# Seven row slots and six diagonals in place of eleven and eight in a product-key retrieval pipeline

## What is computed

```
q = (xb @ w_q)                                   # 8 heads, two halves of 128
s = einsum('bhpc,hpnc->bhpn', q, sub_keys)       # 2 x 128 scores for each head
ts, ti = top_k(s, 16); best_s, pos = top_k(all 256 sums, 16)
idx = cand_i[pos];  gate = softmax(best_s)       # 16 experts of 16384
act = gelu(einsum('bhkd,bd->bhk', u_tab[idx], xb))
out = einsum('bhk,bhkd->bd', gate * act, v_tab[idx])
```

## Time and profile before

| What | us |
|---|---|
| Median of three runs | 3976.35 |
| The profiled execution | 3980.32 |
| Its span | 3978.5 |
| PE busy | 2955.1 |
| DVE busy | 2732.4 |
| ACT busy | 1470.4 |
| POOL busy | 1424.2 |
| Mean rate of the DMA engines | 329 GB/s over the span |

### The profile page before, as it was taken

How to read it: one execution, slowest core, us unless ns; L and a number is a source line. 1 busy time by engine, 2 the same in 40 slices (tenths; PEclk the granted TensorE clock), 3 DMA queues, 4 the chain that set the end, 5 groups by cost and what they waited for, 6 DMA issues and landing times.

```text
span 3978.5 us, 56287 instructions
## 1 busy us (share of the span) xinstructions
PE 2955.1 (74%) x20248; PEld 1449.0 (36%) x20248; DVE 2732.4 (69%) x6352; ACT 1470.4 (37%) x4424; POOL 1424.2 (36%) x1272
## 2 busy tenths in 40 slices
PE   5999999868766666777777766788787676666655
PEld 3777777754222122333333322334342222222111
DVE  5555555546766666778777777889867677777775
ACT  1333333313433333444444433444444343333333
POOL 0001110014444444344444444334444444444442
PEclk8888999889787778888889888999998787787777
DMA  2110000039999999999999999999999999999996
GB/s 79 30 30 26 25 25 25 18 111 425 426 426 427 426 427 426 421 416 399 411 404 426 426 426 425 415 353 369 421 394 427 426 425 427 426 426 426 426 426 289
DMA packets 229640, 1311.06 MB, mean 330 GB/s; under 512 B 58736, under 2 KB 61936, under 8 KB 81648
## 3 DMA queue, kind: packets, MB, share of 16 engines
q0 software_dynamic: 165888, 1208.03, 72.6%
q1 hardware_dynamic: 63472, 99.43, 7.1%
HBM read 1301.52 MB, written 5.86 MB: 329 GB/s over the span
## 4 chain that ended last, share of the span: by engine, by line
DMA 36%; PE 19%; DVE 16%; ACT 3%; issue 3%; DVEq 1%; POOL 1%; ACTq 1%; POOLq 0%
DMA arena<-in_uv,arena 36%; DVE arena L1587 8%; PE psum L1159 8%; PE psum L1121 4%; PE psum L1211 3%; PE psum L1241 2%; DVE arena L1674 1%; POOL arena L1101 1%; ACT wbuf L1377 1%; PE psum L1231 1%; ACT arena L1372 1%; DVE arena L1515 1%; DVE arena L1512 0%; ACT arena L1368 0%; DVE arena L1648 0%
## 5 line engine op out<-in xcount | busy, mean ns | idle before, releaser
L1159 PE MATMUL psum<-arena,wbuf 64*64 64x512 f32 (+1 forms) x8704 | 1451.1, 741 | 865.7 <-ACT wbuf L1377 846.3
L1101 POOL DMA_INDIRECT arena<-in_uv,arena x1152 | 1349.7, 1172 | 1770.7 <-PE psum L1159 1569.4
L1587 DVE SCALAR_TENSOR_TENSOR arena<-arena 128x1024 f32<-128x1024 f32 x1152 | 1396.0, 1222 | 584.9 <-DMA arena<-in_uv,arena 569.6
L1159 PEld LDWEIGHTS psum<-arena,wbuf 64*64 64x64 f32 (+1 forms) x8704 | 335.0, 154 | 1755.5 <-ACT wbuf L1377 1379.3
L1368 ACT ACTIVATE arena<-arena 128x2 f32<-128x2 f32 x576 | 117.0, 203 | 1668.1 <-DVE arena L1587 1663.4
L1377 ACT ACTIVATE wbuf<-cst,arena 128x64 f32<-128x64 f32 x1152 | 338.3, 340 | 41.6 <-issue 2.4
L1121 PE MATMUL psum<-arena,wbuf 128*128 128x256 f32 (+1 forms) x1024 | 312.4, 453 | 8.5 <-DVE arena L1598 5.8
L1372 ACT ACTIVATE arena<-arena 128x1 f32<-128x1 f32 x1152 | 276.8, 287 | 40.9 <-issue 1.4
L1121 PEld LDWEIGHTS psum<-arena,wbuf 128*128 128x128 f32 x1024 | 203.9, 210 | 171.5 <-issue 131.2
L842 POOL COPY arena<-arena 128x256 f32<-128x256 f32 x8 | 3.2, 397 | 584.2 <-DVE arena L735 584.2
L406 PE MATMUL psum<-arena,wbuf 128*128 128x288 f32 x768 | 193.6, 411 | 0.4 <-DMA wbuf<-in_w_rkv 0.4
(11 more groups left out here) (264 smaller groups left out, 3322.9 us busy)
## 6 DMA issues: line engine op xcount, KB each, us to landing
wbuf<-in_w_q SPq DMA_DIRECT2D x64, 576.0 KB, 11.8
arena<-in_w_pw SPq DMA_DIRECT2D x48, 512.0 KB, 8.7
arena<-in_uv,arena POOLq DMA_INDIRECT x1152, 20.3
wbuf<-in_w_rkv SPq DMA_DIRECT2D x24, 512.0 KB, 3.6
wbuf<-in_w_o SPq DMA_DIRECT2D x8, 512.0 KB, 3.7
arena<-in_w_o SPq DMA_DIRECT2D x8, 512.0 KB, 8.5
x<-in_x SPq DMA_DIRECT2D x1, 2304.0 KB, 8.2
arena<-in_state SPq DMA_DIRECT2D x16, 128.0 KB, 3.0
```

The source lines that it names most:

```text
L1101: pool.indirect_dma_start(ring[:, g % RING, :], None, I["uv"][p // 2], bass.IndirectOffsetOnAxis(ap=idx[:, s % 4, j:j + 1], axis=0)).then_ ...
L1159: last = pe.matmul(ps[e * HD:(e + 1) * HD, 2 * (u % 2) + a if u < NB else 4, :], diag[t, g % DIAGS, :], ring[t, g % RING, D + e * 512:D + ...
L1587: stt(out=row, in0=row, scalar=1.0, in1=tok[p % 2][:, UNITS[p % 2].index(u), :], op0=ALU.mult, op1=ALU.mult, accum_out=dots[:, g % COLS:g ...
```

## The change

Two of the constants at the head of `retrieval_and_conv`:

```
-    RING, DIAGS, LEAD, COLS = 11, 8, 2, 12
+    RING, DIAGS, LEAD, COLS = 7, 6, 2, 12
```

## The result

The changed kernel takes 4054.95 us, the median of four runs (4045.47 to 4057.35), against 3976.01 for the kernel before: a ratio of 1.0198, 95% interval 1.0186 to 1.0210. It is slower by 79 us. The forecast was 4045 in a range of 3980 to 4145. The profiled execution took 4053.71 us, 73.4 more than the one before.

The account below looks back on a forecast made before the run. The prediction took transfers at 425 to 427 GB/s to set the pace from slice 9, except in the two convolutions. Its terms, 10 + 28 + 22 + 9 = 69 us on 3980.32, gave 4049, or 4045 for the median; range 3980 to 4145.

Parts of the forecast that it names:

- The loop: Ring at the ceiling: seven slots give 17.8 us; 7.3 outside the DMA engines leaves 10.5 for landing, against 7.1 needed.
- Term 1: Stretches where transfers set the pace, some 1880 us: seven slots mostly suffice, 10 us lost, bounds 0 and 19.
- its own line at 420: Last 900 us: rate still 424 GB/s or more; under 420 the ceiling's term is wrong.
- Term 2: Convolution of half A: four heavy bursts at 5 us and four lighter chunks at 2, 28 us lost, bounds 0 and 78.
- the walk: Row-by-row replay of PE bursts with issues four rows back: half A's row 435 4.6 us late, half B's row 655 9.2.
- The bound of that term: Half A's upper bound: eight times the worth of four slots, 4 x 2.45 = 9.8 us, which is 78 us.
- Term 3: Convolution of half B: 10 us for two PE holds, 2 for each of six other chunks, 22 us lost.
- The first rival: Half B: shorter gather queue speeds SP's weights and stores, up to 78 us gained, 3945 median; chance 0.06.
- Term 4: Three projection stretches around the convolutions: 3 us each, 9 us lost, bounds 0 and 29.
- The diagonals: Wait for row g - 6: ring is the stricter limit, so cost nothing; upper bound 12 us.
- the signs that the text named: Trace checks: landing 10 or 11 us, half A about 385 GB/s, half B 360 to 375, first 880 us within 2 us.
- The prediction's second estimate: Whole kernel: using the skill page's 4.4 us per megabyte instead of the trace's 5.9, some 20 us lower, 4025.

Follow-up runs that it names:

- r11_d6: The kernel before with eleven slots kept and the diagonals cut to six: 3976.3 us, ratio 1.0000.
- r7_gap: The kernel before with seven slots, six diagonals and a four-slot gap keeping every other buffer in its place: 4054.7 us, ratio 1.0199.
- r5_d5: The kernel before with five slots and five diagonals: 4613.7 us, ratio 1.1604.
- The trims: Most weight loads in half A's stage cut to an eighth: 3960.8 us (0.9959) on the kernel before, 4044.5 us (1.0172) on the changed kernel.

## Why the prediction was right, and where its terms were off

The direction, the mechanism and the total hold: it is the slots alone, as r11_d6 and r7_gap show, and the loss is 79 us by the medians (73 by the profiled executions) against 69. That the total came so close is in part luck, since terms were wrong both ways. Step by step:

The loop. The outside part of 7.3 us was read right, and the landing fell to 10.6 where 10 to 11 was said.

Term 1, the ceiling: 10 us said, 12.7 measured over the three stretches. The rate there is 419 in place of 426; the text had put its own line at 420, under which the term would be wrong, and by that line it failed, though the time agrees: that line asked more of the rate than the term did. The other traces with seven slots have 421 and 422 in the same window, and lose 5 to 9 us over the three stretches. Seven slots are close to the edge, as r5_d5 shows, but on the right side.

Term 2, half A: 28 said, 44.4 measured. The mechanism is in the trace; the size was wrong, and in one step, the 5 us for a heavy burst: 20 us for four, where they took 40.7. The 8 for the lighter chunks were 3.7. Row 427 came 0.9 us late by the delay before it (2061.35 - 33.8 - 2026.67, where 33.8 is the delay at row 420), where the walk had 1.1. Row 435 came 2089.76 - 33.8 - 2043.82 = 12.1 late, where the walk had 4.6. It fell short in two ways. It read the delay at row 435, but the worst row is 433: between the two DVE has work of its own that stands in its list, and hands a delay on whole (433 and 435 are both 12.1 late). By the walk's own numbers row 433 lands at 2031.3 + 5 x 2.45 = 2043.5 and its dot began at 2037.10, so 6.4 late. And the walk set each row 2.45 us behind the last. Rows 428 and 429 came 4.6 us apart (2064.38 and 2068.99), with few gathers in flight and no weights yet; from row 431 to 433 they came 3.8 us apart (2075.48 to 2083.03, two rows), in the time in which the weights that SP sends for move (2.2 MB, 5.2 us at 426 GB/s). The trims show that the weights' bytes are a small part of this: without most of them a burst costs about 1 us less. Why gathers that are few in flight land so far apart isn't shown. The bound of that term, four slots' worth or 9.8 us a burst, was the better figure, and three of the four bursts went past it.

Term 3, half B: 22 said, 2.3 measured. The walk started from the 12.16 us hold as if it would still be there. It isn't. The first rival's mechanism, SP's transfers that speed up, was given half of two holds, and in fact it gives back most of what the slots cost: some 8 us lost by the pair without short runs, and 0 to 4 lost with them in five traces over rows 616 to 720. Its sign was there too: weights in under 12 us (10.2 at the median). The prediction said against it that these times don't follow the length of the gathers' queue; in half B, beside short runs, they follow the number of slots. It never came near its price of 78: DVE is busy 317 of 361 us, and a row's time outside the DMA engines fell there from 19.9 to 12.0 us at the same pace.

Term 4, the projections: 9 said, 19.2 measured, 9.5 of it at rows 736 to 768 and 7.9 at rows 456 to 496. In two of the three the four slots' worth of 9.8, the bound, was nearer than the 3 that was taken. No run takes these stages apart.

The diagonals: nothing said, nothing measured. So errors of opposite sign, 16, 10 and 3 us too little in half A, the projections and the ceiling, 20 too much in half B, left the sum near. Of the signs that the text named, the rate of half A fell to 376 GB/s where about 385 was named, and that of half B to 380 where 360 to 375 was; DVE's wait for gathered data rose in both convolutions (from 42 to 78 us over 1640 to 2100, from 5 to 22 over 2490 to 2850); that the time before the first row would stay within 2 us was too tight, it moved by 3.8, and by 9.5 in r11_d6.

The rule of the Trainium skill on turns between queues, in "DMA: Bandwidth & Descriptors", section "Queues, rings and completion order", was used against the first rival. It agrees with half A, where the first projection's weights land in 11.8 us at the median with eleven slots and 11.0 with seven. In half B, beside the short runs, they land in 16.7 and 10.2, so there the rule alone doesn't give SP's times. How much of that is time in which the gathers' queue is empty, and how much is what SP waits for by itself, no run separates.

The prediction's second estimate, 4025, is further off than its sum of 4045: row 427 took 5.7 us from its issue to its dot (2055.66 to 2061.35), near the 5.9 of the earlier trace rows. One reading was slightly off and changes nothing: the first gathers, at 880 us, already fall into slice 8.

## What to carry to other kernels

Before a ring of buffers is cut, work out its loop from the trace, slots times the time per item, less the time from issue to landing; what remains must fit beside the landing of a nearly empty queue, not of the full one. Here 7.3 us outside and 7.1 for the landing, over 2.54 us a row, are 5.7 slots: seven held the pace of the ceiling, five didn't. Then price each burst on the engine that frees the slots at the slots removed times the transfer time of one: 4 x 4 x 2.45 = 39 us here for the four bursts, 44.4 measured in their stage; for two slots 20, of which 12.1 were lost. Read a delay at the worst row, not behind it. And look at what else waits behind those transfers: it may gain, as half B did with nine slots.

## What the runs showed of the hardware

A matmul engine's hold of 12 us "for nothing that the profile shows" was a wait for weights that stood behind short-run transfers in SP's queue: SP's two issues before these weights took 22.52 us beside eleven gather slots, 7.90 beside nine and 1.00 beside seven. The hold was 10.5 to 14.8 us with eleven and twelve slots, under 5 with nine, 3.55 at the most with seven, and it went when the short runs were left out. Four gathers of 1 MB in flight at the median held the rate at 419 GB/s of 426; between two and three held 350.
